# The odd block of a two-stack model: one chunk of depthwise taps on GpSimd, and the layer norm, the turned values and the bias tables placed between the input products

## Time and profile before

| what | us |
|---|---|
| median of three runs (lowest, highest) | 2790.72 (2786.58, 2791.23) |
| the profiled execution | 2796.13 |
| its span, first to last instruction | 2794.4 |
| PE busy in the span | 2633.5 |
| DVE busy | 1688.4 |
| ACT busy | 1133.1 |

### The profile page before, as it was taken

One profiled execution on the slowest core, in us unless ns is written; L12 is line 12 of the kernel. 1 busy time (PEld: TensorE's weight loads), 2 busy tenths in 40 slices (PEclk: granted clock), 3 DMA queues, 4 the chain that ended last, 5 costly groups with the idle time before them and its releaser, 6 DMA issues.

```text
span 2794.4 us, 34688 instructions
## 1 busy us (share of the span) xinstructions
PE 2633.5 (94%) x13246; PEld 2080.8 (74%) x13246; DVE 1688.4 (60%) x3265; ACT 1133.1 (41%) x2065; POOL 0.2 (0%) x4
## 2 busy tenths in 40 slices
PE   7998999999999999988999999999999999999898
PEld 5876878668888768678886688886876666787565
DVE  6755556455446776565654644468476675598654
ACT  4235444433232232454435432223336675232553
POOL 0000000000000000000000000000000000000000
PEclk9989999999999999899999999999999999999999
DMA  4310023113226522100331132365110000122311
GB/s 147 100 57 16 1 98 121 53 61 106 97 94 205 178 66 94 56 8 16 111 124 39 61 106 99 97 230 174 46 46 16 16 16 23 53 77 75 63 52 45
DMA packets 73506, 219.36 MB, mean 78 GB/s; under 512 B 21248, under 2 KB 21504, under 8 KB 72576
## 3 DMA queue, kind: packets, MB, share of 16 engines
q1 hardware_dynamic: 48384, 176.29, 19.5%
q10 hardware_dynamic: 24960, 40.87, 4.6%
HBM read 215.03 MB, written 2.10 MB: 78 GB/s over the span
## 4 chain that ended last, share of the span: by engine, by line
PE 70%; DVE 17%; ACT 6%; issue 5%; ACTq 1%; DMA 0%; DVEq 0%; SPq 0%
PE bank L575 17%; PE bank L576 17%; PE bank L577 17%; PE bank L789 4%; DVE mod_part L2521 3%; PE bank L753 3%; DVE c_y L2033 3%; PE bank L763 3%; DVE w_lo L541 2%; ACT w_hi L534 2%; PE bank L1214 1%; PE bank L1222 1%; DVE hT L724 1%; PE bank L1160 1%; DVE e_s L848 1%
## 5 line engine op out<-in xcount | busy, mean ns | idle before, releaser
L575 PE MATMUL bank<-a_hi,w_hi 128*128 128x512 f32 (+1 forms) x1552 | 620.9, 400 | 35.6 <-DVE a_lo L671 18.6
L577 PE MATMUL bank<-a_hi,w_lo 128*128 128x512 f32 (+1 forms) x1552 | 611.5, 394 | 0.0
L576 PE MATMUL bank<-a_lo,w_hi 128*128 128x512 f32 (+1 forms) x1552 | 611.1, 394 | 0.0
L534 ACT ACTIVATE w_hi<-w_raw 128x1024 fp32r<-128x1024 f32 x334 | 352.6, 1060 | 570.1 <-PE bank L577 460.7
L541 DVE TENSOR_TENSOR w_lo<-w_raw,w_hi 128x1024 fp32r<-128x1024 f32 x334 | 407.5, 1223 | 271.8 <-ACT w_hi L534 270.8
L575 PEld LDWEIGHTS bank<-a_hi,w_hi 128*128 128x128 f32 (+1 forms) x1552 | 293.9, 189 | 120.2 <-issue 32.2
L577 PEld LDWEIGHTS bank<-a_hi,w_lo 128*128 128x128 f32 (+1 forms) x1552 | 293.8, 189 | 64.4
L576 PEld LDWEIGHTS bank<-a_lo,w_hi 128*128 128x128 f32 (+1 forms) x1552 | 294.0, 189 | 63.9 <-issue 2.7
L575 PE MATMUL bank<-b_hi,w_hi 128*128 128x512 f32 x752 | 275.3, 366 | 4.4 <-DVE b_lo L737 3.4
L576 PE MATMUL bank<-b_lo,w_hi 128*128 128x512 f32 x752 | 266.5, 354 | 0.0
L577 PE MATMUL bank<-b_hi,w_lo 128*128 128x512 f32 x752 | 265.3, 353 | 0.0
(11 more groups left out here) (378 smaller groups left out, 3881.5 us busy)
## 6 DMA issues: line engine op xcount, KB each, us to landing
w_raw<-w_tiles SPq DMA_DIRECT2D x334, 512.0 KB, 3.5
mod_raw<-mod_tiles ACTq DMA_DIRECT2D x48, 512.0 KB, 3.5
d_bias<-rpb_rows ACTq DMA_DIRECT2D x16, 224.0 KB, 4.4
hT<-xT ACTq DMA_DIRECT2D x4, 512.0 KB, 11.2
m_in<-memT ACTq DMA_DIRECT2D x2, 1024.0 KB, 4.7
mod_cond<-cond_rows ACTq DMA_DIRECT2D x2, 1024.0 KB, 6.6
out<-hT ACTq DMA_DIRECT2D x8, 256.0 KB, 2.2
ctx_sq<-ctxT ACTq DMA_DIRECT2D x1, 1024.0 KB, 7.7
```

Source lines behind the costliest of these rows:

```text
L534: act.activation(w_hi[:, t % SPLIT, :], w_raw[:, t % RAW, :], ACT.Copy).then_inc(sem("w_rounded"), 1)
L575: pe.matmul(o, wh, hi[:, k, :n], start=k == 0, stop=False)
L576: pe.matmul(o, wh, lo[:, k, :n], start=False, stop=False)
L577: mm = pe.matmul(o, wl, hi[:, k, :n], start=False, stop=k == kc - 1)
```

## The change

- DVE works the taps of chunks 0, 2 and 3. GpSimd works those of chunk 1 (`conformer_pool`): the gate, then for each tap a `tensor_scalar` into one of two scratch rows and a `tensor_tensor` that adds it to `c_y`. A tap that was one instruction is two there. GpSimd also adds the four finished chunks into one row, and later the four squares, so that each channel sum on PE is one matmul in place of four.
- The mean is taken after product dq0, together with the turning of the values; the variance after product dq2. ACT and DVE do their parts of the layer norm in the same places. The mean's division is folded into the centring.
- The bias tables of heads 0 and 1 and the column mask are loaded after product cl1, those of heads 2 and 3 after dq0; the mask is added to the first two right after the centring.
- The layer norm's scratch rows lie in `d_pt`. The eight `warm_pe` matmuls before the attention are left out.

```diff
+                if name == MEAN_AFTER:
+                    odd_turn_pe(pe)
+                    conformer_mean_pe(pe)
+                if name == VAR_AFTER:
+                    conformer_var_pe(pe)
...
+        MEAN_AFTER, VAR_AFTER = "dq0", "dq2"
...
-                    act.wait_ge(*when("c_in", i - 1))
+                    act.wait_ge(*when(*glu_done(i - 1)))
...
+                if name == "cl1":
+                    act.wait_ge(*when("bank_filled", "rstd", "m2", 1, "lat"))
+                    for h in range(2):
+                        load_bias(act, h)
+                    act.dma_start(col_mask[:, :], dram["column_mask"]).then_inc(*loaded("col_mask"))
+                if name == MEAN_AFTER:
+                    odd_turn_act(act)
+                    for i in range(CC):
+                        act.wait_ge(*when(*taps_done(i)))
+                    for h in range(2, 4):
+                        load_bias(act, h)
+                    load_sqrt_act(act)
+                    conformer_squares_act(act)
+                if name == VAR_AFTER:
+                    conformer_std_act(act)
+            conformer_silu_act(act)
+
+        POOL_C = 1
+        ln_flat = d_pt[:, :, :, :].rearrange("p l k q -> p (l k q)")
+        ln_row = ln_flat[:, 5 * S:6 * S]
+
+        def ln_sq(c):
+            return ln_flat[:, S * (c + 1):S * (c + 2)]
+
+        def glu_done(c):
+            return ("c_in_pool",) if c == POOL_C else ("c_in", c)
+
+        def taps_done(c):
+            return ("c_tap_pool", CT - 1) if c == POOL_C else ("c_tap", c, CT - 1)
 
         def conformer_taps_dve(dve):
 
             side = CT // 2
...
+                if c == POOL_C:
+                    continue
...
+        def conformer_pool(pool):
...
+            c, side = POOL_C, CT // 2
+            pool.wait_ge(*when("c_zero", CC - 1, 1))
+            pool.wait_ge(*when("shifted_in", 1, "ctx", KC - 1))
+            pool.wait_ge(*when("c_val", c))
+            pool.wait_ge(*when("c_glu", c))
+            u = c_u[:, c, side:side + S]
+            pool.tensor_tensor(u, u, c_g[:, c, :], ALU.mult).then_inc(*done("c_in_pool"))
+            pool.wait_ge(*when("c_in_pool"))
+            pool.tensor_scalar(c_y[:, c, :], c_u[:, c, 0:S], G("dw_w", CT * c), G("dw_b", c), ALU.mult, ALU.add)\
+                .then_inc(*done("c_tap_pool", 0))
+            for j in range(1, CT + 1):
+                if j < CT:
+                    if j > 2:
+                        pool.wait_ge(*when("c_tap_pool", j - 2))
+                    pool.tensor_scalar(ln_sq(j % 2), c_u[:, c, j:j + S], G("dw_w", CT * c + j), None, ALU.mult)\
+                        .then_inc(*done("c_part_pool", j))
+                if j > 1:
+                    pool.wait_ge(*when("c_part_pool", j - 1))
+                    pool.wait_ge(*when("c_tap_pool", j - 2))
+                    pool.tensor_tensor(c_y[:, c, :], c_y[:, c, :], ln_sq((j - 1) % 2), ALU.add)\
+                        .then_inc(*done("c_tap_pool", j - 1))
+            pool.wait_ge(*when("c_tap_pool", CT - 1))
+            for i in range(1, CC):
+                pool.wait_ge(*when(*taps_done(i)))
+                if i == 1:
+                    pool.wait_ge(*when(*taps_done(0)))
+                else:
+                    pool.wait_ge(*when("c_summed", i - 1))
+                pool.tensor_tensor(ln_row, c_y[:, 0, :] if i == 1 else ln_row, c_y[:, i, :], ALU.add)\
+                    .then_inc(*done("c_summed", i))
+            for i in range(1, CC):
+                pool.wait_ge(*when("c_sq", i))
+                if i > 1:
+                    pool.wait_ge(*when("c_sq_summed", i - 1))
+                pool.tensor_tensor(ln_sq(0), ln_sq(0), ln_sq(i), ALU.add).then_inc(*done("c_sq_summed", i))
+
         def conformer_dve(dve):
...
-            for _ in taps:
...
+                if name == MEAN_AFTER:
+                    for _ in taps:
+                        pass
+                    b = bank(dve, "c_sum")
+                    for c in range(CC):
+                        op = dve.scalar_tensor_tensor(out=c_y[:, c, :], in0=b[:, :], scalar=-1.0 / (CC * P),
+                                                      in1=c_y[:, c, :], op0=ALU.mult, op1=ALU.add)
+                        op.then_inc(*(freed("c_sum", also=("c_centred", c)) if c == CC - 1
+                                      else done("c_centred", c)))
+                    bias_dve(dve, 0)
+                if name == VAR_AFTER:
+                    dve.wait_ge(*when("c_std"))
+                    dve.reciprocal(ln_row, ln_row).then_inc(*done("c_rstd"))
+                    dve.wait_ge(*when("c_rstd"))
+                    for c in range(CC):
+                        dve.scalar_tensor_tensor(out=c_y[:, c, :], in0=c_y[:, c, :], scalar=G("ln_g", c), in1=ln_row,
+                                                 op0=ALU.mult, op1=ALU.mult).then_inc(*done("c_scaled", c))
+
+        def conformer_mean_pe(pe):
...
-            for c in range(CC):
-                pe.wait_ge(*when("c_tap", c, CT - 1))
-                mm = pe.matmul(b[:, :], ones, c_y[:, c, :], start=c == 0, stop=c == CC - 1)
-            mm.then_inc(*filled("c_sum"))
+            pe.wait_ge(*when("c_summed", CC - 1))
+            pe.matmul(b[:, :], ones, ln_row, start=True, stop=True).then_inc(*filled("c_sum"))
...
+        def conformer_var_pe(pe):
...
-                pe.wait_ge(*when("c_sq", c))
-                mm = pe.matmul(b[:, :], ones, sq[:, c % 2, :], start=c == 0, stop=c == CC - 1)
-                mm.then_inc(*(filled("c_var") if c == CC - 1 else done("c_sq_used", c)))
-
-        def conformer_act(act):
+            pe.wait_ge(*when("c_sq_summed", CC - 1))
+            pe.matmul(b[:, :], ones, ln_sq(0), start=True, stop=True).then_inc(*filled("c_var"))
...
+        def conformer_squares_act(act):
...
-                if c >= 2:
-                    act.wait_ge(*when("c_sq_used", c - 2))
-                act.activation(sq[:, c % 2, :], c_y[:, c, :], ACT.Square).then_inc(*done("c_sq", c))
+                act.activation(ln_sq(c), c_y[:, c, :], ACT.Square).then_inc(*done("c_sq", c))
...
+        def conformer_std_act(act):
...
-            act.activation(spread[:, :], b[:, :], ACT.Sqrt, bias=C("eps"), scale=1.0 / (CC * P))\
+            act.activation(ln_row, b[:, :], ACT.Sqrt, bias=C("eps"), scale=1.0 / (CC * P))\
...
-            if h == 0:
-                act.wait_ge(*when("c_silu", CC - 1))
...
         def bias_dve(dve, u):
...
-            if u % (2 * TT):
+            if u % (2 * TT) or ("bias", u // TT) in bias_added:
                 return
+            bias_added.add(("bias", u // TT))
...
-            conformer_pe(pe)
-            odd_turn_pe(pe)
-            warm_pe(pe, 8, "odd_att")
...
-            conformer_act(act)
-            odd_turn_act(act)
-            for h in range(4):
-                load_bias(act, h)
-            act.dma_start(col_mask[:, :], dram["column_mask"]).then_inc(*loaded("col_mask"))
...
+        @block.gpsimd
+        def _(pool):
+            conformer_pool(pool)
```

More of the change, by code:

```diff
@@ L2053, in conformer_dve @@
                         next(taps, None)
-            for _ in taps:
-                pass
-            b = bank(dve, "c_sum")
-            dve.wait_ge(*when("c_tap", CC - 1, CT - 1))
-            dve.tensor_scalar(sqacc[:, :], b[:, :], 1.0 / (CC * P), None, ALU.mult)\
-               .then_inc(*freed("c_sum", also=("c_mean",)))
-            dve.wait_ge(*when("c_mean"))
-            for c in range(CC):
-                dve.tensor_tensor(c_y[:, c, :], c_y[:, c, :], sqacc[:, :], ALU.subtract).then_inc(*done("c_centred", c))
@@ L2063, in conformer_dve @@
-            dve.wait_ge(*when("c_std"))
-            dve.reciprocal(spread[:, :], spread[:, :]).then_inc(*done("c_rstd"))
-            dve.wait_ge(*when("c_rstd"))
-            for c in range(CC):
-                dve.wait_ge(*when("c_centred", c))
-                dve.scalar_tensor_tensor(out=c_y[:, c, :], in0=c_y[:, c, :], scalar=G("ln_g", c), in1=spread[:, :],
-                                         op0=ALU.mult, op1=ALU.mult).then_inc(*done("c_scaled", c))
-        def conformer_pe(pe):
+                if name == MEAN_AFTER:
[8 more added lines that the diff above has]
+                    bias_dve(dve, 0)
@@ L2139, in odd_units @@
             return units
+        bias_added = set()
         def bias_dve(dve, u):
-            if u % (2 * TT):
+            if u % (2 * TT) or ("bias", u // TT) in bias_added:
                 return
+            bias_added.add(("bias", u // TT))
             for h in (u // TT, u // TT + 1):
```

3 lines of the change are left out of this document (1 added, 2 removed).

## The result

| | before | after |
|---|---|---|
| median of 17 runs each, side by side (us) | 2794.64 | 2801.88 |
| lowest, highest | 2786.58, 2798.39 | 2795.10, 2807.42 |
| ratio, 95% interval | | 1.0031 [1.0023, 1.0040] |
| span of the profiled execution | 2794.4 | 2800.2 |
| gate of chunk 0 on DVE, the start of the taps | 2455.87 | 2452.70 |

By the ratio the change makes the kernel 0.31% slower, 8.7 us; the two medians lie 7.2 us apart. Executions differ in when they reach the odd block (the first gate lies between 2446 and 2457 us in the profiles of this study, whatever the kernel), so I count from DVE's first gate. From there to the end the profile after is 9.0 us longer: 5.6 up to the first maximum, 3.4 behind it.

The account below looks back on a forecast made before the run. PE bounds the whole, a serial chain the odd block. Taps ready at 2542.4 + 57.0, then additions 2.8, mean 0.96 and 20.2 to the first maximum: about +20 us, median 2811; own range 2799 to 2825, for all 2762 to 2824.

Parts of the forecast that it names:

- added by the instructions on GpSimd: Beside DVE's taps: 62 GpSimd instructions of 0.92 us each cost DVE their whole time, 57.0 us.
- x: Microseconds that one GpSimd instruction adds to the taps' end; taken as 0.92, range 0.75 to 1.15.
- mean to first maximum: From the mean's end through products dq1 to dq3 to the attention's first maximum: 17.3 + 2.9 = 20.2 us.
- first exponential later than before by: At the attention's start, ACT's silus and table loads delay its first exponential, costing up to 2.5 us.
- DMA issues behind cl1: Five loads on ACT's queue ahead of cv2's evacuation, up to 6 us; taken as 0, 1.5 if cover fails.
- rival 2: DVE and GpSimd share reads, each GpSimd instruction adds half of 0.92, 0.46 us: -10 us, median 2781; chance 0.09.
- The break-even of the formula: First maximum at 2563.5 + 65 x, equal to the kernel before at x = 0.62, faster below it.
- Rival 1: GpSimd runs beside DVE's taps at no cost: first maximum 2576.6, -26 us, median 2765; chance 0.33.
- Rival 3: GpSimd merely slow at 1.9 us an instruction, no disturbance of DVE: -1.5 us, median 2789; chance 0.05.
- the sum is within 3 us the same: Taps' end at 2599.4 us, within 3 us, whether DVE and GpSimd alternate or GpSimd waits until DVE is through.
- tap distance: Start to start of DVE's taps between 2458 and 2560 us: 0.79 before, about 1.7 where alternating with GpSimd.
- The clock: PE enters the attention without the pause where its clock was granted at 0.66, giving about 1 us back.

Follow-up runs that it names:

- kernel 3: The changed kernel with taps 1 to 30 of chunk 1 left out, so GpSimd works only gate, tap 0 and sums; 2768.17 us, ratio 0.9932 to before.
- kernel 6: The changed kernel with DVE's taps added up in a held PSUM bank in place of c_y; 2776.60 us, ratio 0.9956 to before.
- kernels 3 and 4: The second: the changed kernel with GpSimd's 60 instructions of taps 1 to 30 replaced by fills that only write; 2769.26 us, ratio 0.9933 to before.
- kernel 5: The changed kernel with GpSimd's 30 two-input additions replaced by one-input products, sum over taps not formed; 2799.87 us, ratio 1.0033 to before.
- kernel 11: The changed kernel with DVE's taps in PSUM and chunk 1 shared, GpSimd taps 0 to 22, DVE the last 8; 2770.43 us, ratio 0.9929 to before.
- kernel 12: The changed kernel with GpSimd's 30 one-input products in two-operation form, adding a column of zeros; 2804.07 us, ratio 1.0058 to before.
- kernel 7: The kernel before, no GpSimd taps, with DVE's taps added up in a held PSUM bank; 2794.62 us, ratio 1.0013 to before.

## Why the prediction was right, and where its sizes were off

The side was right (slower), and so was the mechanism: two-input work on DVE and reads on GpSimd get in each other's way out of SBUF, and DVE has no slack. The size was not: 20 us were forecast, and 8.7 came, just under the forecast's own range of 9 to 35. The median came at 2801.9, where 2811 was forecast; by the ratio on the median of 2790.7 that the forecast started from it is 2790.7 x 1.0031 = 2799.4. Step by step, from the first gate:

| step | forecast (us) | measured | |
|---|---|---|---|
| DVE's 93 taps and its splits, undisturbed | 86.6 | 89.7 | in kernel 3, whose 2 instructions of the chunk left add to it |
| added by the instructions on GpSimd | 57.0 | 38.0 | 127.7 - 89.7; x is 38.0 / 60 = 0.63, or (127.7 - 86.6) / 62 = 0.66, not 0.92 |
| last tap to end of the mean | 3.8 | 4.4 | additions 2.20 for the last |
| mean to first maximum | 20.2 | 21.4 | |
| gate to first maximum | 167.5 | 153.6 | |
| first exponential later than before by | 2.5 | 2.5 | 4.02 against 1.55 |
| DMA issues behind cl1 | 0 | 0 | cv2 moved out at 2458.41 |

The mis-sized term is x. I had taken the whole duration of a GpSimd instruction, guessed from DVE's, as time that DVE loses. Two errors stand in that, with opposite signs. The durations were too low: an addition takes 1.28 us undisturbed and a product 1.57 (in kernel 6 beside taps that do not contend), not 0.92. And DVE does not lose all of it: 0.91 with the addition, 0.31 with the product, 0.61 in the mean of the two. That is 0.43 of their mean of 1.43 us, nearer to the half of rival 2 than to the whole; rival 2 forecast a gain only because it took the half of the short duration.

The sign was in part luck. The break-even of the formula is x = 0.62, and the measured 0.63 lies on it, below the forecast's own range of 0.75 to 1.15. With 38.0 us in place of 57.0 the prediction's own sum puts the first maximum 148.6 us after the gate, 0.6 later than before. The other 5.0 us up to the first maximum are small terms that the sum had too short (3.1 for the undisturbed taps, 0.6 to the mean, 1.2 to the maximum), and 3.4 more stand behind it, which no run explains. The chances (0.51 slower, 0.41 faster) said how close it was.

Rival 1 had the undisturbed order right: 120.7 forecast, 123.2 and 122.4 in kernels 3 and 4. Rival 3, GpSimd merely late, did not happen in the change (GpSimd waited 3.8 us for DVE before its last addition), but it did in kernel 5 and mildly in kernel 6. The prediction's claim that the sum is within 3 us the same, whether DVE and GpSimd take turns or GpSimd is held back, is not shown: kernel 5 has its centring at 131.4 us after the gate against 132.2, but it changed the work on GpSimd as well.

The forecast for the tap distance was "about 1.7 where it alternates with GpSimd": it is 1.19, three taps to a pair of instructions, because GpSimd's are longer than I took and so come less often. PE waited for w_lo in the cv to dv products, 21.3 us in ten waits, as forecast. The clock did what I had counted on between the last tap and the first maximum, where it was granted at 1.00 (0.66 and 0.95 in the pause before). But it fell to 0.91 in the starved products ahead of that, where before it was 1.00, and this the sum had not counted.

## What to carry to other kernels

Work given to a second engine pays only if the first does not lose more than it hands over: here each tap moved took 0.79 us from DVE and cost it 1.22 elsewhere, since both read SBUF, and moving DVE's accumulator to PSUM turned 0.31% slower into 0.44% faster. Before any of that, look at the wait that ends last: moving five DMA issues earlier gave 0.36% with none of the rest. And once the contention is gone, share a serial job so that both engines end together (0.44% faster became 0.71%).

## What the runs showed of the hardware

- On GpSimd a one-input product of 128x512 f32 with one operation takes 1.57 us undisturbed, more than an addition of two inputs (1.28). With two operations, the second adding a column of zeros, the single instruction of that form in kernel 11 took 0.77 and the 30 in kernel 12, beside DVE's taps, 1.40 on the mean. Fills take 0.53. The Trainium skill (GPSIMD Engine Reference, section Elementwise — side-by-side cycle accounting) has 0.77 us as the best case, for a tight loop over 512 elements, which the second form meets and the first does not; why, no run tells.
- What a GpSimd instruction adds to DVE's two-input taps, by its kind: 0 for a fill, 0.31 us for a one-input read, 0.91 for two inputs. The price did not fall as the instruction was shortened (kernel 12).
- A one-input `tensor_scalar` of DVE from SBUF to SBUF took 0.55 us alone and 1.40 beside an addition of GpSimd (kernel 3); with its output in PSUM it took 0.81 alone (kernel 7) and 0.81 beside GpSimd (kernel 6).
- At a split of 1024 elements either engine can be the one that waits: GpSimd in the rows of the change shown (a product of 2.94 for 1.89, the split 1.21), DVE at others (its splits have a mean of 1.46 there, of 1.57 in kernel 6 and 1.75 in kernel 12, against 1.22 before). I can't say what decides.
